# Raw tiles turned as they land, the RMS norm applied to the weights and to the products

## The reference

```python
def rms_norm(x, g):
    xf = x.astype(jnp.float32)
    y = xf * lax.rsqrt(jnp.mean(xf * xf, axis=-1, keepdims=True) + EPS)
    return (y * g.astype(jnp.float32)).astype(x.dtype)

z = rms_norm(x, norm_g) @ w_in          # 2048 -> 6144 columns, [B | C | x_in | q | k | v]
u = c_gate * x_in
y = sum(conv_w[j] * u_ext[:, j:j + T] for j in range(CONV_WIDTH))
return b_gate * y, u_ext[:, -(CONV_WIDTH - 1):]
```

## Time and profile before

| | |
|---|---|
| median of 3 runs | 3629.45 us (3622.49 to 3636.41) |
| the profiled execution's own time | 3624.97 us |
| its span, from the first to the last instruction | 3623.2 us |
| granted TensorE clock, mean | 0.97 |
| norm stage, from the start to the first matmul of the projection | 73.4 us |
| projection, from there to its last turn | 1191 us |

### The profile page before, as it was taken

The page is one execution under the profiler, slowest core; times in us unless marked ns, Lnnn a source line. Parts: engine busy times, 40 slices in busy tenths (PEclk is TensorE's granted clock), DMA queues, the critical chain, the costliest instruction groups (busy, mean ns, idle before and its releaser), DMA issues. The chain is left out here.

```text
span 3623.2 us, 51079 instructions
## 1 busy us (share of the span) xinstructions
PE 3369.6 (93%) x18429; PEld 2949.8 (81%) x18430; DVE 1671.1 (46%) x1742; ACT 1291.2 (36%) x1581; POOL 838.9 (23%) x689
## 2 busy tenths in 40 slices
PE   7999999999999987989999959999999999999990
PEld 6999999999999965667888847878888778778770
DVE  5211112100111146871021168558888858846677
ACT  4000000000000034660011137557878757746572
POOL 2222222222222111224445431111111111101010
PEclk9999999999999998999999969999999999999995
DMA  4112111222222292116354459769999969967798
GB/s 154 59 54 67 54 59 54 68 65 79 86 77 66 69 348 96 53 47 226 120 163 154 130 197 351 268 239 354 358 368 354 379 240 374 360 236 258 266 338 358
DMA packets 340683, 692.65 MB, mean 191 GB/s; under 512 B 23034, under 2 KB 150954, under 8 KB 329983
## 3 DMA queue, kind: packets, MB, share of 16 engines
q1 hardware_dynamic: 290340, 586.79, 45.8%
q10 hardware_dynamic: 37163, 66.14, 4.9%
q0 software_dynamic: 13104, 38.69, 3.0%
HBM read 638.29 MB, written 97.28 MB: 203 GB/s over the span
## 5 line engine op out<-in xcount | busy, mean ns | idle before, releaser
L1900 DVE TENSOR_TENSOR e_w_lo<-expert_raw,e_w_hi 128x2048 fp32r<-128x2048 f32 x388 | 872.5, 2287 | 253.8 <-ACT e_w_hi L1812 226.2
L1812 ACT ACTIVATE e_w_hi<-expert_raw 128x2048 fp32r<-128x2048 f32 x388 | 744.4, 1919 | 301.8 <-PE e_gu L1726 253.1
L280 PE MATMUL p_z<-hT_hi,p_w_hi 128*128 128x384 f32 x2256 | 755.0, 335 | 1.6 <-DVE p_xs L399 1.6
L282 PE MATMUL p_z<-hT_hi,p_w_lo 128*128 128x384 f32 x2256 | 753.6, 334 | 0.0
L281 PE MATMUL p_z<-hT_lo,p_w_hi 128*128 128x384 f32 x2256 | 753.6, 334 | 0.0
L280 PEld LDWEIGHTS p_z<-hT_hi,p_w_hi 128*128 128x128 f32 x2256 | 423.6, 188 | 1.9 <-DVE p_xs L399 1.9
L281 PEld LDWEIGHTS p_z<-hT_lo,p_w_hi 128*128 128x128 f32 x2256 | 423.6, 188 | 0.0
L282 PEld LDWEIGHTS p_z<-hT_hi,p_w_lo 128*128 128x128 f32 x2256 | 423.5, 188 | 0.0
L1726 PE MATMUL e_gu<-e_w_hi,e_xT_hi 128*128 128x512 f32 x1216 | 390.2, 392 | 6.2 <-issue 6.2
L1726 PE MATMUL e_gu<-e_w_hi,e_xT_lo 128*128 128x512 f32 x1216 | 387.5, 390 | 0.0
L1726 PE MATMUL e_gu<-e_w_lo,e_xT_hi 128*128 128x512 f32 x1216 | 387.4, 390 | 0.0
(11 more groups left out here) (327 smaller groups left out, 4519.1 us busy)
## 6 DMA issues: line engine op xcount, KB each, us to landing
expert_raw<-w_ei SPq DMA_DIRECT2D x256, 1024.0 KB, 8.5
expert_raw<-w_eo SPq DMA_DIRECT2D x128, 1024.0 KB, 10.4
p_w_raw<-w_in SPq DMA_DIRECT2D x96, 512.0 KB, 3.9
m_w_raw<-w_out SPq DMA_DIRECT2D x64, 512.0 KB, 4.2
d_v<-cache_v SPq DMA_DIRECT2D x8, 2048.0 KB, 8.3
rows_back<-expert_rows SPq DMA_DIRECT2D x12, 1024.0 KB, 15.8
n_x<-x SPq DMA_DIRECT2D x9, 1024.0 KB, 5.1
chunks<-p_e ACTq DMA_DIRECT2D x16, 576.0 KB, 2.8
```

Of the source, the lines that this page charges most:

```text
L280: pe.matmul(out, w_hi[:, k, :], x_hi[:, xk, cols], start=(k == 0), stop=False)
L282: mm = pe.matmul(out, w_lo[:, k, :], x_hi[:, xk, cols], start=False, stop=(k == KT - 1))
L1812: act.activation(w_hi[:, s, :], raw[:, r, :], ACT.Copy).then_inc(hi_done, 1)
L1900: dve.tensor_tensor(w_lo[:, s, :], raw[:, r, :], w_hi[:, s, :], ALU.subtract).then_inc(lo_done[r], 1)
```

## The change

The tile is no longer multiplied before it is turned. TensorE turns the raw tile as soon as it has landed. The vector g (loaded as 16 rows of 128 and turned by one transpose into `gain`, one number per partition and slice) is multiplied into the raw weights by GpSimd, a third operation ahead of each half's split. ScalarE squares tile t-1 behind tile t's high parts, and takes all 9 roots in one instruction at the end; VectorE inverts them, spreads them over 1152 columns (`wide`), TensorE turns that by 9 transposes, and VectorE keeps it as `rstd_row`, the same row of 1152 factors on all partitions. In the projection each copy out of PSUM becomes a multiplication by this row; the convolution has two more multiplications of 128x1152, because its u is a product of two projections and the row is applied to both sides. `n_x` has four places instead of three, and a place comes free when its tile has been squared. In the last block's products the small transposes stand after 8 slices and the 9 new ones after 12.

```diff
+                def load_tile(t):
+                    if t >= XS:
+                        sp.wait_ge(squared, t - XS + 1)
+                    sp.dma_start(x[:, t % XS, :], io.x[t * P:(t + 1) * P, :]).then_inc(x_loaded[t % XS], 16)
+                load_tile(0)
+                sp.dma_start(g_rows, io.norm_mix.rearrange("o (k n) -> (o k) n", k=KT)).then_inc(g_loaded, 16)
+                load_tile(1)
+                load(sp, 0, lambda half: w[half, :, :, 2 * DC:2 * DC + P], (0,))
+                load_tile(2)
+                load(sp, 0, lambda half: w[half, :, :, 2 * DC:2 * DC + P], (1,))
+                for t in range(3, NT):
+                    load_tile(t)
                 load(sp, 1, lambda half: w[half, :, :, DC:DC + P])
-                sp.wait_ge(x_done[0], NT // SL + 1)
+                sp.wait_ge(squared, 6)
...
+                pool.wait_ge(c.gain_kept, 1)
...
+                def square(t):
+                    act.activation(x[:, t % XS, :], x[:, t % XS, :], ACT.Square, accum_out=ssq[:, t:t + 1]).then_inc(squared, 1)
+                def keep_hi(t):
...
+                act.wait_ge(ident_step, 3)
+                act.activation(lw[:, 7:8], c.eps[:], ACT.Sqrt)
+                keep_hi(0)
+                for t in range(1, NT):
+                    keep_hi(t)
+                    square(t - 1)
+                square(NT - 1)
+                act.wait_ge(squared, NT)
+                act.activation(ssq[:], ssq[:], ACT.Sqrt, bias=c.eps[:], scale=1.0 / D).then_inc(squared, 1)
...
-                def scale(s, i, t):
-                    dve.wait_ge(ms_done, t + 1)
-                    dve.reciprocal(rstd[:, s:s + 1], ssq[:, s:s + 1]).then_inc(rstd_done, 1)
-                    dve.wait_ge(rstd_done, t + 2)
-                    dve.scalar_tensor_tensor(x[:, s, :], x[:, s, :], rstd[:, s:s + 1], g[:], ALU.mult,
-                                             ALU.mult).then_inc(h_ready, 1)
...
+                dve.wait_ge(g_turned, 1)
+                dve.tensor_copy(c.gain[:], tp[:, 3, 0:KT]).then_inc(c.gain_kept, 1)
+                for t in range(NT):
+                    keep_lo(t)
...
+                dve.wait_ge(squared, NT + 1)
+                dve.reciprocal(rstd[:], ssq[:]).then_inc(rstd_step, 1)
+                dve.wait_ge(rstd_step, 1)
+                dve.tensor_copy(wide, rstd[:].unsqueeze(2).to_broadcast([P, NT, P])).then_inc(rstd_step, 1)
+                for b in range(NB):
+                    dve.wait_ge(rstd_turned, b + 1)
+                    dve.tensor_copy(c.rstd_row[:, b * BLK:(b + 1) * BLK], tp[:, b, 0:BLK])
...
+                def turn(t):
+                    pe.wait_ge(x_loaded[t % XS], 16 * (t // XS + 1))
                     for q in range(4):
-                        pe.wait_ge(lo_done, 4 * t + 1)
+                        if t > 0:
+                            pe.wait_ge(lo_done, 4 * (t - 1) + q + 1)
+                        elif q == 3:
+                            pe.wait_ge(c.gain_kept, 1)
...
+                pe.wait_ge(lo_done, 4 * NT)
+                first_products(pe, NB - 1, range(0, 8), z, hT_hi, hT_lo)
                 pe.wait_ge(small_loaded, 16)
-                pe.wait_ge(lo_done, 4 * NT + 1)
                 for j in range(CH):
-                    mm = pe.transpose(tp[:, 0, j * 19:(j + 1) * 19], small[:, j * P:(j + 1) * P], c.ident[0:19, 0:19])
+                    mm = pe.transpose(tp[:, 3, j * 19:(j + 1) * 19], small[:, j * P:(j + 1) * P], c.ident[0:19, 0:19])
                 mm.then_inc(small_turned, 1)
-                first_products(pe, NB - 1, range(KT), z, hT_hi, hT_lo)
+                first_products(pe, NB - 1, range(8, 12), z, hT_hi, hT_lo)
+                pe.wait_ge(rstd_step, 2)
+                for b in range(NB):
+                    for j in range(NB):
+                        mm = pe.transpose(tp[:, b, j * P:(j + 1) * P], wide[:, b * NB + j, :], c.ident[:])
+                    mm.then_inc(rstd_turned, 1)
+                first_products(pe, NB - 1, range(12, KT), z, hT_hi, hT_lo)
...
-        pool.tensor_copy(w_hi[:, part, :], w_raw[:, part, :]).then_inc(hi_done, 1)
-        pool.wait_ge(hi_done, 2 * n + half + 1)
+        pool.tensor_tensor(w_raw[:, part, :], w_raw[:, part, :], c.gain[:, part].unsqueeze(2).to_broadcast([P, HALF, P]),
+                           ALU.mult).then_inc(step, 1)
+        pool.wait_ge(step, 4 * n + 2 * half + 1)
+        c.hold(pool)
+        pool.tensor_copy(w_hi[:, part, :], w_raw[:, part, :]).then_inc(step, 1)
+        pool.wait_ge(step, 4 * n + 2 * half + 2)
...
-                        dve.tensor_copy(xs[:, b * BLK:(b + 1) * BLK], z[:, b, 0:BLK]).then_inc(z_kept[b], 1)
+                        dve.tensor_tensor(xs[:, b * BLK:(b + 1) * BLK], z[:, b, 0:BLK], row[:, b * BLK:(b + 1) * BLK],
+                                          ALU.mult).then_inc(z_kept[b], 1)
...
+                    dve.tensor_tensor(xs[:], xs[:], row[:], ALU.mult).then_inc(step, 1)
...
-                        dve.tensor_scalar(e[:, b * BLK:(b + 1) * BLK], z[:, b, 0:BLK], SCALE, None, ALU.mult).then_inc(z_kept[b], 1)
+                        dve.scalar_tensor_tensor(e[:, b * BLK:(b + 1) * BLK], z[:, b, 0:BLK], SCALE, row[:, b * BLK:(b + 1) * BLK],
+                                                 ALU.mult, ALU.mult).then_inc(z_kept[b], 1)
```

More of the change, by code:

```diff
@@ L97, in sems, with phase_turn @@
         return [self.sem(f"{name}{i}") for i in range(n)]
-def one_ahead(eng, front, back):
-    front(0, 0, 0)
-    with eng.Fori(0, NT // SL - 1) as i:
-        for s in range(SL):
-            front((s + 1) % SL, i + (s + 1) // SL, i * SL + s + 1)
-            back(s, i * SL + s)
-    for s in range(SL):
-        if s + 1 < SL:
-            front(s + 1, NT // SL - 1, NT - SL + s + 1)
-        back(s, NT - SL + s)
-def phase_norm(c, hT_hi, hT_lo, z, chunks_of_weights):
+def phase_turn(c, hT_hi, hT_lo, z, chunks_of_weights):
     nc, io, sem = c.nc, c.io, c.sem
+    XS = 4
     with ExitStack() as mem:
-        x = mem.enter_context(nc.sbuf_tensor("n_x", [P, SL, D], F32))
-        g = mem.enter_context(nc.sbuf_tensor("n_g", [P, D], F32))
-        ssq = mem.enter_context(nc.sbuf_tensor("n_ssq", [P, SL], F32))
-        rstd = mem.enter_context(nc.sbuf_tensor("n_rstd", [P, SL], F32))
-        small = x[0:19, 0, 0:DC]
+        x = mem.enter_context(nc.sbuf_tensor("n_x", [P, XS, D], F32))
+        ssq = mem.enter_context(nc.sbuf_tensor("n_ssq", [P, NT], F32))
+        rstd = mem.enter_context(nc.sbuf_tensor("n_rstd", [P, NT], F32))
+        lw = mem.enter_context(nc.sbuf_tensor("n_lw", [P, 8], F32))
+        g_rows = c.rstd_row[0:KT, 0:P]
+        small = x[0:19, 1, 0:DC]
+        lamb = x[:, 1, DC:DC + 4 * DH]
+        wide = x[:, 2, 0:TOK].rearrange("p (t n) -> p t n", t=NT)
         load, split_half, _, first_products, _, _, first_counts = chunks_of_weights
@@ L139, in _ @@
             def _(sp):
[L140 to L147 removed]
+                def load_tile(t):
[10 more added lines that the diff above has]
+                    load_tile(t)
                 load(sp, 1, lambda half: w[half, :, :, DC:DC + P])
[L149 removed]
+                sp.wait_ge(squared, 6)
                 sp.dma_start(small, io.small).then_inc(small_loaded, 16)
[L151 removed]
+                sp.dma_start(lamb, io.lam.to_broadcast([P, 4 * DH])).then_inc(lam_loaded, 16)
                 sp.dma_start(c.hn[:], io.head_norm.to_broadcast([P, VD])).then_inc(lam_loaded, 16)
@@ L234, in _ @@
+                pe.wait_ge(g_loaded, 16)
+                pe.transpose(tp[:, 3, 0:KT], g_rows, c.ident[0:KT, 0:KT]).then_inc(g_turned, 1)
+                for t in range(NT):
+                    turn(t)
                     b = t // SL - 1
                     if b >= 0:
-                        pe.wait_ge(lo_done, 4 * SL * (b + 1) + 1)
+                        pe.wait_ge(lo_done, 4 * SL * (b + 1))
                         first_products(pe, b, PIECES[t % SL], z, hT_hi, hT_lo)
+                pe.wait_ge(lo_done, 4 * NT)
@@ L252, in weight_chunks, with load @@
     z_done, z_kept = c.sems(f"{tag}_z_done", NB), c.sems(f"{tag}_z_kept", NB)
-    def load(sp, n, w_cols):
-        for half in range(2):
+    def load(sp, n, w_cols, halves=(0, 1)):
+        for half in halves:
             sp.wait_ge(split[half], n + 1)
@@ L392, in _ @@
                 es = slice(2, 2 + NEW)
-                STEPS = 10
+                STEPS = 12
+                row = c.rstd_row
                 dve.wait_ge(zeroed, 1)
@@ L429, in _ @@
                         dve.scalar_tensor_tensor(ys, us[:, :, j:j + NEW], tap(j), ys, ALU.mult, ALU.add).then_inc(step, 1)
+                    dve.wait_ge(step, t * STEPS + 11)
+                    dve.tensor_tensor(xs[:], xs[:], row[:], ALU.mult).then_inc(step, 1)
                     dve.wait_ge(step, t * STEPS + STEPS)
@@ L464, in keep_e @@
                         dve.wait_ge(z_done[b], m + NQ + 2)
[L465 removed]
```

(2 more changed lines are left out.)

84 lines of the change are left out of this document (29 added, 55 removed).

## The result

The changed kernel takes 3610.6 us (median of 6 runs, 3606.97 to 3619.23), the one before 3629.05 us over the same comparison: a ratio of 0.9952, 95% interval 0.9942 to 0.9963, so 13 to 21 us less. A second comparison gave 3614.64 against 3627.05 us, 0.9959 (0.9945 to 0.9972). Both intervals hold the 14 us that the trace shows: TensorE's first matmul of the projection starts at 59.33 us, where it started at 73.38. The profiled execution itself took 3616.81 us, span 3614.5.

The account below looks back on a forecast made before the run. TensorE, busy 93% of the span, was taken as the bound. Projection start 47.8 + 10.8 + 1.6 + 2.1 = 62.3 instead of 73.4 us, 11.1 off the median 3629.45, gives 3618.4 us; range 3607 to 3630.

Parts of the forecast that it names:

- the head: Norm stage, first to fourth tile: TensorE turns raw tiles early, ScalarE then sets the pace, fourth turn ends at 20.5 us.
- the middle: Norm stage, fourth to ninth tile: TensorE is the bound without waits, 27.3 us, third block begins at 47.8 us.
- the tail: Third block to projection: 10.8 us as before, plus 1.6 for transposes and switches and 2.1 waiting for the spread roots.
- The early first turn: Start of the norm stage: TensorE needs only the raw tile and g, first turn at 6.7 us instead of 13.82.
- None of them is late by more than a few tenths: First loads: tiles 1 to 3 and both halves of the first weights land in time, tile 3 at about 17 us.
- the spreading copy behind the cast: End of the norm stage: VectorE's 128x1152 copy of the roots is excluded until GpSimd's cast ends, done at T + 9.2.
- 2.1 or 4.5, never 0: TensorE's wait for the spread roots: by the shared-pair lock 2.1 us, or 4.5 if GpSimd's subtraction gets in first.
- GpSimd's multiplication: New operation on each weight half, taken at 2.38 us (1.04 to 4.8), hidden in the projection under TensorE's 12.4 us.
- Rival 1: No wait for the roots, as exclusion spares the spreading copy or it wins the gaps: 13.2 us off, 3616; chance 0.20.
- Rival 2: First tiles give back more, by longer slow clock, late tiles or longest wait: 6 us off, 3623; chance 0.17.
- Rival 3: GpSimd bounds the projection if its multiplication passes 8.8 us; at 10 us the kernel takes about 3731; chance 0.04.
- Rival 4: More than 18 us off, only by scatter, since the projection cannot start before about 57 us; chance 0.03.

Follow-up runs that it names:

- tile 3 first: The changed kernel with tile 3 loaded ahead of half 1 of the first weights: projection starts at 57.0 us, run 3606.08 us.
- the last kernel: The changed kernel with tile 3 loaded before half 1 of the first weights and roots spread before the small transposes' copy: median 3607.78 us, 0.9948 of the kernel before.

## Why the prediction was right, and where its sizes were off

Forecast were 3618.4 us and 11.1 off; it came to 3610.6, and 14.05 off in the stage. Range and direction hold, and the reason is the one given: TensorE alone carries the projection, so what leaves the norm stage leaves the kernel. The sizes were 3.0 us too cautious: 0.5 in the head, 1.3 in the middle, 1.2 in the tail. The median moved 4.4 us more than the stage, and that part is scatter as far as is known.

- *The early first turn.* Forecast 6.7, measured 6.49. g was there with tile 0.
- *The head.* Forecast: the fourth turn ends at 20.5, no tile late. Measured: products start at 20.03, but by another road. The transposes went to the faster pace during the second turn (two turns took 5.78 us, not 7.1), and TensorE then stood 2.21 us, about the last 1 of them for tile 3 alone. "None of them is late by more than a few tenths" failed: tile 3 came at 17.1 as computed, but TensorE was done with tile 2 at 14.9 and could have gone on at about 16.1, when the first low part of tile 2 was done. The turn that followed then ran at 0.50, 1.3 us longer than at 1.00. A start that was too late in the forecast and a slow turn that was not in it cancelled: that the head came out right is luck. ScalarE's pace, which was to rule here, ruled only where tile 3 is early (tile 3 first: 18.10).
- *The middle.* Forecast 27.3 us, measured 46.01 - 20.03 = 25.98. The term mis-sized is the turn with its switch, 2.06 us each; it is 1.66, since the changed code no longer waits for its own transposes to be counted before the products. The diff shows that line gone; the prediction gave it no price. The wait put back shows 0.3 us of the 0.4; the remaining 0.1 was not traced. Five turns give 2.0 us less, and 0.7 went back into the pieces of products, 0.5 of it in the first, which began at 0.50 (23.17 - 20.03 = 3.14 us instead of 2.68).
- *The tail.* Forecast 3.7 us more (1.6 and 2.1), measured 2.5 more: 1.20 for the transposes, 1.20 for the wait. The step that failed is the spreading copy behind the cast. The exclusion is real for the small product of two SBUF operands (1.35 us against 0.28) and not for the copy with a broadcast source, which takes 1152 elements at 1.17 ns each, 1.35 us, beside a multiplication, beside a cast and alone. The rule quoted from the Trainium skill (SBUF — State Buffer, Who interferes with whom) speaks of a copy in a two-port mode. This copy's rate (1.35 us for 1152 elements, against 0.74 for the 1024 of the tensor_scalar in the earlier trace rows) says that it is not in one, and so the trace agrees with the rule as it is written; the prediction had assumed the mode. The 1.20 us of waiting come from the product that stands ahead of the copy. "2.1 or 4.5, never 0" was too strong: with the product out of the way the wait is 0.
- *GpSimd's multiplication.* Taken at 2.38, bounds 1.04 and 4.8, measured 1.90. The projection's 1190.9 us are those of before, as forecast. The limit of 12.4 us a half lies between the 8.0 that cost no wait and the 13.0 that did.
- *Rivals.* Rival 1 had the reason right (the exclusion does not touch the spreading copy) and the outcome wrong (there was a wait, of 1.2 us, by the product ahead of it); its 13.2 us off are nearer to the measured 14.05 than the forecast's 11.1. Rival 2 did not come. Rival 3 is refuted for this kernel and real at 13 us. Rival 4 (more than 18 us) is met by the first comparison's median, 18.4, and not by the second's 12.4 nor by the stage's 14.05. Its bound for the start of the projection (about 57) was 1 us too high: the last kernel starts at 56.0, since a turn with its switch costs 1.66 us and the first two together 5.8.

The median moved 18.4 us in the first comparison and 12.4 in the second. The 4 us beyond the stage's 14 in the first are not shown to come from the change.

## What to carry to other kernels

A factor per row or per column of an operand can be moved past a product, and the value is not the operations saved but the engine that no longer has to wait for them: here 7.3 us of first wait and the loop between three engines. What it is moved onto is free only as far as a cover reaches that can be counted from the trace (8.0 us of GpSimd a half cost no wait here, 13.0 did). At a stage's barrier no cover may be left. When a chain of waits is cut, look for what is next in line: here the order of VectorE's last operations was worth 1.5 us, the order of the first transfers 2.3 and one more buffer 4.4, nearly a third of the gain.
